# End of the mixing stage in another order: mLSTM scores in the rotary banks, output-weight products between the last heads

## The chip, the cores and the metric

The kernel runs on one core of a Trainium2 chip. The metric is device time in microseconds (us), lower is better: the median over executions.

## The reference, cut to what matters

Two layers of a streaming encoder, 256 tokens, 1024 wide, float32. Each layer has a SwiGLU, a mixing stage, a memory cross-attention and a second SwiGLU, with a layer norm behind each. The mixing stage joins three head groups and multiplies them by one output matrix:

```python
a_out = diff_attention(dq, dk, dv, lam)            # 4 heads, columns 0..511
h = mlstm_chunkwise(q, k, v, ig, lf)               # 4 heads, columns 512..767
b_out = sigmoid(mo) * rms_norm(h, mlstm_norm_g)
c_out = s5_layer(su, ...)                          # columns 768..1023
return jnp.concatenate([a_out, b_out, c_out], -1) @ w_out
```

The memory's keys and values, `mem @ wkv`, do not depend on x and can be computed at any time.

## The kernel before

Every float32 weight block ("unit") of 1 MB (0.5 MB for those in `HALF`) is loaded by SP into one of 5 slots (`RING`), split by ScalarE (ACT) into a high part `WH` and by VectorE (DVE) into a low part `WL` (`split`, once on each engine per unit), and used by TensorE (PE) in three products high x high, high x low, low x high (`prod`). All engines walk through the units in the one order of `unit_order`: unit u is loaded when unit u-5 has been used (`unit_used`), and a `split()` on ACT or DVE always takes the next unit. Each engine is a queue in order; waits are semaphores written by hand.

The end of `mix(l)` on PE works in eight PSUM banks. Banks 0 to 3 become the sum of the output product. `diff_scores`, `diff_turn`, `diff_out` are scores, transposes of probabilities and output of one differential head (heads 0, 1, 3 in banks 6 and 7, head 2 in 4 and 5). `spread` and `decay` give the mLSTM gate matrix `SDA`; `mlstm_scores(h)` multiplies q and k of head h, DVE multiplies that by `SDA` (`decay_scores`, event `msd_ready`), `mlstm_num` multiplies by the values, `mlstm_sums` and `mlstm_scale` (DVE, with a root on POOL) make `CATM` (event `b_ready`). `turn_cat` transposes finished pairs of column blocks, and `cat_high` (ACT) and `cat_low` (DVE) write them to `CH` and `CL`, the inputs of the output product. Output weights are the units W0 (block 6), W1 (block 7), W2 (0, 1), W3 (4, 5), W4 (2, 3). Blocks 6 and 7 are the S5 group, 0 to 3 the heads, 4 and 5 the mLSTM.

`FILL` places products of the memory's keys and values between these steps: in the mixing stage of layer 0 four of them, called `mid` 0 to 3 (units K2, K3, V0, V1); in layer 1 none. `mid_out` evacuates such a product on ACT, and `mid_split(l, i)` is a split that exists in layer 0 alone.

At the end POOL loads the next norm's parameters (`load_gb`, tile `LNGB`), 0.5 MB twice.

Of the kernel before, what the change touches and what calls it, by code (L numbers as in the profile page):

```python
# [35 lines left out]
HEADS = 4  # L36
# [4 lines left out]
TAPS = 4  # L41
# [20 lines left out]
def unit_order():  # L62

    order = []
    for l in range(DEPTH):
        order += [(l, "F0", i) for i in range(FFN_UNITS)]
        order += FILL["mix", l]
        order += [(l, "DV", 0), (l, "DV", 1), (l, "DQ", 0), (l, "DK", 0), (l, "SU", 0), (l, "MQ", 0), (l, "MK", 0),
                  (l, "DQ", 1), (l, "DK", 1), (l, "MM", 0), (l, "MM", 1)]
        mid = FILL["mid", l]  # L70
        order += mid[0:3] + [(l, "W", i) for i in range(4)] + mid[3:4] + [(l, "W", 4)]
        order += FILL["xattn", l]
        order += [(l, "WQ", i) for i in range(4)]
        order += [(l, "WO", i) for i in range(5)]
        order += FILL["ffn2", l]
        order += [(l, "F1", i) for i in range(FFN_UNITS)]
        order += FILL["next", l]
    return order
# [32 lines left out]
def build(nc, x_in, mem_in, wg, wu, wd, ln_g, ln_b, w_in, w_out, wq, wkv, wo, par, const, out):  # L111
# [12 lines left out]
    with ctx:  # L124
# [34 lines left out]
        UT = sb("UT", [P, 2, SEQ])  # L159
# [220 lines left out]
        def _(sp):  # L380
# [59 lines left out]
            for l in range(DEPTH):  # L440
# [11 lines left out]
                for half in range(2):  # L452
                    load_rows(UNIT[l, "MM", half], win_v, l, 4 * half, slice(C_MV, C_MV + 512))
                load_fill("mid", l, 0, 3)
                load_single(UNIT[l, "W", 0], wout_v, l, 6)
                load_single(UNIT[l, "W", 1], wout_v, l, 7)
                load_pair(UNIT[l, "W", 2], wout_v, l, 0)
                load_pair(UNIT[l, "W", 3], wout_v, l, 4)
                load_fill("mid", l, 3, 4)
# [20 lines left out]
        def _(pe):  # L480
# [271 lines left out]
            def mlstm_scores(l, h):  # L752
# [3 lines left out]
                if h < 2:  # L756
                    pe.wait_ge(decay_done.sem, decay_done.at(l, 2 * h + 2))
                else:
                    pe.wait_ge(msd_ready.sem, msd_ready.at(l, h - 1))
                b = h % 2  # L760
                k = COUT[:, 2 + h // 2, :]
# [5 lines left out]
            def mlstm_num(l):  # L767
                pe.wait_ge(msd_ready.sem, msd_ready.at(l, HEADS))
                for t in range(TT):
                    for h in range(HEADS):  # L770
                        o = PS[:, 2 + t, h * 65:h * 65 + 65]
                        if t == 0:
# [105 lines left out]
            def mix(l):  # L878
# [48 lines left out]
                diff_scores(l, 1)  # L927
                cols(l)

                s5_scatter(l)  # L930
                unit_ready(UNIT[l, "MM", 1])
                form_a_tile(UNIT[l, "MM", 1], 1, 0, XH, XL, 0)
                pe.wait_ge(ut_ready.sem, ut_ready.at(l, 2))
                for f in range(2):
# [18 lines left out]
                diff_out(l, 2)  # L953
                diff_scores(l, 3)
                mlstm_scores(l, 2)
                mlstm_scores(l, 3)
                fill_read("mid", l, 1)
                mlstm_num(l)
                diff_turn(l, 3)
                pe.wait_ge(a_ready.sem, a_ready.at(l, 1))  # L960
                pe.wait_ge(do_read.sem, do_read.at(l, 3))
                turn_cat(l, CATA, 0, 5)
                mid(l, 2, 4)
                diff_out(l, 3)

                pe.wait_ge(c_lo.sem, c_lo.at(l, 1))
                pe.wait_ge(num_read.sem, num_read.at(l, 1))
                w = UNIT[l, "W", 0]
                rows_product(w, [6], CH, CL, True, False)
                rows_product(w + 1, [7], CH, CL, False, False)  # L970
                pe.wait_ge(cat_lo.sem, cat_lo.at(l, 1))
                pe.wait_ge(b_ready.sem, b_ready.at(l, 1))
                turn_cat(l, CATM, 0, 5)
                rows_product(w + 2, [0, 1], CH, CL, False, False)
                pe.wait_ge(cat_lo.sem, cat_lo.at(l, 2))
                rows_product(w + 3, [4, 5], CH, CL, False, False)
                fill_read("mid", l, 2)
                mid(l, 3, 4)
                pe.wait_ge(a_ready.sem, a_ready.at(l, 2))
                turn_cat(l, CATA, 2, 7)  # L980
                pe.wait_ge(cat_lo.sem, cat_lo.at(l, 3))
# [91 lines left out]
        def _(act):  # L1073
# [210 lines left out]
            def mix(l):  # L1284
# [41 lines left out]
                split()  # L1326
                act.wait_ge(cols_done.sem, cols_done.at(l, 1))
                copy(SM[:, 184:200], PS[:, 3, 0:16]).then_inc(cols_read.sem, 1)
                diff_exp(l, 1)
# [3 lines left out]
                for f in range(2):  # L1333
                    g = nc.scalar.activation(ZG[:, f, :], PS[:, 2, f * SEQ:f * SEQ + SEQ], ACT.Sigmoid,
                                             bias=PAR[:, P_GLUB + f:P_GLUB + f + 1])
                g.then_inc(glu_sig.sem, 1)
                act.wait_ge(va_ones.sem, va_ones.at(l, 1))
                for t in range(TT):
                    act.wait_ge(unit_used.sem, UNIT[l, "MM", 1] + 1)
                    copy(VA[:, t, :, 0:64], PS[:, t, 0:256].rearrange("p (h d) -> p h d", h=HEADS))  # L1340
                    nc.scalar.activation(SIGO[:, t, :], PS[:, t, 256:512], ACT.Sigmoid).then_inc(mm_read.sem, 1)
                diff_turned(l, 1)
                split()
                diff_exp(l, 2)
                act.wait_ge(cols_read.sem, cols_read.at(l, 1))
# [4 lines left out]
                diff_evac(l, 1)  # L1350
                act.wait_ge(c_hi_in.sem, c_hi_in.at(l, 1))
                copy(CH[:, 6:8, :].rearrange("p f (k s) -> p f k s", s=TAPS),
                     UT[:, :, :].rearrange("p f (s k) -> p f k s", s=TAPS)).then_inc(c_hi.sem, 1)
                split()
                diff_turned(l, 2)
                mid_out(l, 1, 3)
                diff_evac(l, 2)
                split()
                diff_exp(l, 3)
                diff_turned(l, 3)  # L1360
                cat_high(l, 0, 0, 5)
                mid_out(l, 2, 4)
                diff_evac(l, 3)
                mid_split(l, 3)
                cat_high(l, 1, 4, 5)
                split()
                mid_out(l, 3, 4)
                cat_high(l, 2, 2, 7)
                split()
# [73 lines left out]
        def _(dve):  # L1443
# [251 lines left out]
            def decay_scores(l, h):  # L1695

                dve.wait_ge(decay_done.sem, decay_done.at(l, h + 1))
                dve.wait_ge(ms_done.sem, ms_done.at(l, h + 1))
                v.scalar_tensor_tensor(SDA[:, h, :], PS[:, h % 2, 0:384], 0.125, SDA[:, h, :],
                                       ALU.mult, ALU.mult).then_inc(msd_ready.sem, 1)  # L1700

            def mlstm_sums(l):

                dve.wait_ge(num_done.sem, num_done.at(l, 2))
                dve.wait_ge(exp_m.sem, exp_m.at(l, 1))
                n8 = PS[:, 2:4, 0:260].rearrange("p t (h d) -> p t h d", h=HEADS)
                den = SM[:, 120:128]
# [91 lines left out]
            def mix(l):  # L1799
# [48 lines left out]
                diff_combine(l, 2)  # L1848
                diff_max(l, 3)
                decay_scores(l, 2)  # L1850
                decay_scores(l, 3)
                split()
                mlstm_sums(l)
                mlstm_scale(l)
                cat_low(l, 0, 0, 5)
                diff_sums(l, 3)
                diff_combine(l, 3)
                diff_stats(l, 1)
                mid_split(l, 3)
                diff_norm(l, 1)  # L1860
                cat_low(l, 1, 4, 5)
                split()
                cat_low(l, 2, 2, 7)
                split()
# [354 lines left out]
```

## Time and profile before

| | us |
|---|---|
| median of 3 runs (1332.24 to 1340.2) | 1333.86 |
| the profiled execution | 1331.73 |
| its span, first to last instruction | 1329.9 |
| mean granted TensorE clock | 0.986 |
| PE busy | 1266.2 (95%) |
| PE weight load busy | 1084.9 (82%) |
| DVE busy | 772.8 (58%) |
| ACT busy | 590.9 (44%) |

"Busy" is the share of the span in which the engine has an instruction in work. The chain of work that ended last is 72% PE. The mixing stage of layer 0 ends its output product near 398 us, that of layer 1 near 1044 us.

### The profile page before, as it was taken

What the parts mean: (1) busy time and instruction counts of PE and PEld (TensorE: products, weight loads), DVE (VectorE), ACT (ScalarE), POOL (GpSimd) and SP (SyncE); (2) the same over time, 40 slices, a digit from 0 to 9 for tenths busy, and PEclk for the clock granted to TensorE, in tenths of its full rate; (3) what the DMA queues carried; (4) which work ended last, traced back from release to release, by engine and by line L of the source; (5) the groups of instructions that cost most, each with busy time, mean ns of one, the idle gap of its engine ahead of it and who ended that gap; (6) DMA issues with size and microseconds to landing.
All of it is one profiled execution on the core that took longest, in us unless ns stands there. A gap on an engine that the chain in (4) does not pass through costs nothing.

```text
span 1329.9 us, 16421 instructions
## 1 busy us (share of the span) xinstructions
PE 1266.2 (95%) x6896; PEld 1084.9 (82%) x6896; DVE 772.8 (58%) x1003; ACT 590.9 (44%) x670; POOL 151.8 (11%) x153
## 2 busy tenths in 40 slices
PE   6999999999999999999999999999998898999997
PEld 5788888897888888888887878888987796788885
DVE  5577646585545555544556686466747646455543
ACT  5444553456433545444444445544454444344441
POOL 1008800000100000000001088000001000000000
PEclk8999999999899999999999999999999999999999
DMA  8755555421254355555547555545232534455550
GB/s 278 246 186 176 186 183 165 159 96 64 95 191 158 127 190 192 188 190 190 190 158 266 188 174 181 186 159 158 84 107 96 174 112 158 158 190 190 190 189 33
DMA packets 160041, 219.46 MB, mean 165 GB/s; under 512 B 6848, under 2 KB 136000, under 8 KB 159968
## 3 DMA queue, kind: packets, MB, share of 16 engines
q1 hardware_dynamic: 156544, 205.61, 46.2%
q0 software_dynamic: 3152, 11.76, 2.5%
q8 instruction: 54, 0.88, 0.3%
q10 hardware_dynamic: 272, 1.05, 0.2%
q14 instruction: 19, 0.16, 0.0%
HBM read 217.34 MB, written 1.05 MB: 164 GB/s over the span
## 4 chain that ended last, share of the span: by engine, by line
PE 72%; issue 16%; DVE 5%; DMA 3%; ACT 3%; SPq 0%; POOL 0%; DVEq 0%; POOLq 0%; ACTq 0%
PE PS L485 21%; PE PS L487 21%; PE PS L486 21%; DMA RAW<-in_ffn_w_up 2%; DVE WL L1455 1%; ACT WH L1075 1%; PE PS L516 1%; PE PS L996 1%; PE PS L1020 1%; ACT XH L1075 1%; PE PS L553 1%; PE PS L692 1%; DMA RAW<-in_w_out 1%; PE PS L790 0%; DMA RAW<-in_w_in 0%
## 5 line engine op out<-in xcount | busy, mean ns | idle before, releaser
L1455 DVE TENSOR_TENSOR WL<-RAW,WH 128x2048 fp32r<-128x2048 f32 (+1 forms) x198 | 448.3, 2269 | 278.9 <-ACT WH L1075 278.5
L1075 ACT ACTIVATE WH<-RAW 128x2048 fp32r<-128x2048 f32 (+1 forms) x198 | 370.5, 1878 | 182.3 <-DMA RAW<-in_ffn_w_up 132.7
L485 PE MATMUL PS<-WH,XH 128*128 128x512 f32 x768 | 307.4, 400 | 16.2 <-ACT XH L1075 6.5
L487 PE MATMUL PS<-WH,XL 128*128 128x512 f32 x768 | 300.8, 392 | 0.0
L486 PE MATMUL PS<-WL,XH 128*128 128x512 f32 x768 | 300.6, 391 | 0.0
L485 PEld LDWEIGHTS PS<-WH,XH 128*128 128x128 f32 x768 | 145.2, 189 | 47.5 <-issue 10.8
L487 PEld LDWEIGHTS PS<-WH,XL 128*128 128x128 f32 x768 | 144.9, 189 | 30.9
L486 PEld LDWEIGHTS PS<-WL,XH 128*128 128x128 f32 x768 | 145.3, 189 | 28.7 <-issue 0.5
L485 PE MATMUL PS<-WH,HH 128*128 128x512 f32 x352 | 138.7, 394 | 4.6 <-issue 4.6
L486 PE MATMUL PS<-WL,HH 128*128 128x512 f32 x352 | 137.6, 391 | 0.0
L487 PE MATMUL PS<-WH,HL 128*128 128x512 f32 x352 | 137.5, 391 | 0.0
L485 PE MATMUL PS<-XH,WH 128*128 128x256 f32 x352 | 103.7, 295 | 3.2 <-ACT XH L1075 3.2
L486 PE MATMUL PS<-XL,WH 128*128 128x256 f32 x352 | 99.5, 283 | 0.0
L487 PE MATMUL PS<-XH,WL 128*128 128x256 f32 x352 | 99.5, 283 | 0.0
L1075 ACT ACTIVATE HH<-PS 128x512 fp32r<-128x512 f32 x44 | 26.2, 596 | 142.2 <-PE PS L516 142.2
L2098 POOL TENSOR_TENSOR SM<-SM,half_c 128x2 f32<-128x2 f32 x8 | 5.7, 711 | 695.3 <-DVE SM L1507 695.3
L485 PEld LDWEIGHTS PS<-WH,HH 128*128 128x128 f32 x352 | 66.5, 189 | 20.3 <-issue 6.8
L1151 ACT ACTIVATE SG<-PS 128x256 f32<-128x256 f32 x88 | 33.5, 383 | 110.0 <-PE PS L487 109.8
L487 PEld LDWEIGHTS PS<-WH,HL 128*128 128x128 f32 x352 | 66.5, 189 | 14.1
L486 PEld LDWEIGHTS PS<-WL,HH 128*128 128x128 f32 x352 | 66.5, 189 | 13.5
L485 PEld LDWEIGHTS PS<-XH,WH 128*128 128x128 f32 x352 | 67.3, 191 | 5.7 <-ACT XH L1075 3.7
L1455 DVE TENSOR_TENSOR HL<-PS,HH 128x512 fp32r<-128x512 f32 x44 | 30.3, 689 | 69.8 <-ACT HH L1075 69.6
(318 smaller groups left out, 1786.0 us busy)
## 6 DMA issues: line engine op xcount, KB each, us to landing
RAW<-in_ffn_w_gate SPq DMA_DIRECT2D x88, 512.0 KB, 3.8
RAW<-in_ffn_w_up SPq DMA_DIRECT2D x88, 512.0 KB, 4.8
RAW<-in_ffn_w_down SPq DMA_DIRECT2D x88, 512.0 KB, 4.3
RAW<-in_w_in SPq DMA_DIRECT2D x44, 512.0 KB, 4.3
RAW<-in_xattn_wkv SPq DMA_DIRECT2D x32, 512.0 KB, 4.1
RAW<-in_xattn_wq SPq DMA_DIRECT2D x16, 512.0 KB, 3.9
RAW<-in_w_out SPq DMA_DIRECT2D x12, 512.0 KB, 4.4
RAW<-in_xattn_wo SPq DMA_DIRECT2D x12, 512.0 KB, 3.9
```

The source lines that it names most:

```text
L485: nc.tensor.matmul(out_ap, sh, mh, start=first, stop=False)
L486: nc.tensor.matmul(out_ap, sh, ml, start=False, stop=False)
L487: return nc.tensor.matmul(out_ap, sl, mh, start=False, stop=last)
L516: mm = nc.tensor.transpose(PS[:, 6, fc * SEQ + t * P:fc * SEQ + t * P + P], HB[:, t, fc * P:fc * P + P], ident)
L553: mm = nc.tensor.transpose(PS[:, 4 + 2 * t + half, i * P:i * P + P], X[:, t, c * P:c * P + P], ident)
L692: mm = nc.tensor.matmul(PS[0:32, 7, j * P:j * P + P], PCB[:, o:o + 32], CQ[:, part, i, 0:TAPS, :].rearrange("p a c -> p (a c)"), start=(pa ...
L996: mm = nc.tensor.matmul(PS[:, h, t * SEQ:t * SEQ + SEQ], QX[:, 2 * h + c, t * P:t * P + P], KT[:, 2 * h + c, :], start=(c == 0), stop=(c = ...
L1020: mm = nc.tensor.matmul(PS[:, 6 + h % 2, dc * SEQ:dc * SEQ + SEQ], V[:, mt, (2 * h + dc) * P:(2 * h + dc + 1) * P], XPT[:, h % 2, mt, :], ...
L1075: return nc.scalar.activation(dst, src, ACT.Copy)
L1151: nc.scalar.activation(SG[:, t, :], PS[:, 4 + t, 0:FB], ACT.Silu).then_inc(sg_done.sem, 1)
L1455: return v.tensor_tensor(dst, full, hi.bitcast(F32), ALU.subtract)
L2098: g.tensor_tensor(SM[:, 22:24], SM[:, 20:22], half_c[:, 0:2], ALU.pow).then_inc(ln_root.sem, 1)
```

## The change

No operation is added or taken away; they are put in another order and in other banks.

- `mlstm_scores` of heads 2 and 3 go to banks 4 and 5 instead of 0 and 1, and wait for head 2's output to be read; `mlstm_num` goes to 4 and 5 instead of 2 and 3.
- On PE, W0 follows `diff_out(l, 2)`, then the transposes of heads 0 and 1, scores 2 and 3, `diff_scores(l, 3)`, W1, `mlstm_num`, `diff_turn(l, 3)`, the first half of W2, `diff_out(l, 3)`, the transposes of `CATM`, the second half of W2, `mid` 2, half of W3, the last transposes, the other half of W3, `mid` 3, and W4.
- `cols` moves behind the first tile of unit MM 1, and its evacuation on ACT behind the sigmoids.
- The unit V0 moves from before W0 to between W2 and W3, in loads and splits alike.
- On ACT and DVE splits, evacuations, `cat_high`, `cat_low` and the decay products are put in the matching order.

```diff
@@ -70,3 +70,3 @@
         mid = FILL["mid", l]
-        order += mid[0:3] + [(l, "W", i) for i in range(4)] + mid[3:4] + [(l, "W", 4)]
+        order += mid[0:2] + [(l, "W", i) for i in range(3)] + mid[2:3] + [(l, "W", 3)] + mid[3:] + [(l, "W", 4)]
         order += FILL["xattn", l]
@@ -453,3 +453,3 @@
                     load_rows(UNIT[l, "MM", half], win_v, l, 4 * half, slice(C_MV, C_MV + 512))
-                load_fill("mid", l, 0, 3)
+                load_fill("mid", l, 0, 2)
                 load_single(UNIT[l, "W", 0], wout_v, l, 6)
@@ -457,2 +457,3 @@
                 load_pair(UNIT[l, "W", 2], wout_v, l, 0)
+                load_fill("mid", l, 2, 3)
                 load_pair(UNIT[l, "W", 3], wout_v, l, 4)
@@ -758,4 +759,4 @@
                 else:
-                    pe.wait_ge(msd_ready.sem, msd_ready.at(l, h - 1))
-                b = h % 2
+                    pe.wait_ge(do_read.sem, do_read.at(l, 3))
+                b = (0, 1, 4, 5)[h]
                 k = COUT[:, 2 + h // 2, :]
@@ -770,3 +771,3 @@
                     for h in range(HEADS):
-                        o = PS[:, 2 + t, h * 65:h * 65 + 65]
+                        o = PS[:, 4 + t, h * 65:h * 65 + 65]
                         if t == 0:
@@ -927,3 +928,2 @@
                 diff_scores(l, 1)
-                cols(l)
 
@@ -932,2 +932,3 @@
                 form_a_tile(UNIT[l, "MM", 1], 1, 0, XH, XL, 0)
+                cols(l)
                 pe.wait_ge(ut_ready.sem, ut_ready.at(l, 2))
@@ -953,29 +954,31 @@
                 diff_out(l, 2)
-                diff_scores(l, 3)
+                w = UNIT[l, "W", 0]
+                pe.wait_ge(c_lo.sem, c_lo.at(l, 1))
+                pe.wait_ge(msd_ready.sem, msd_ready.at(l, 2))
+                fill_read("mid", l, 1)
+                rows_product(w, [6], CH, CL, True, False)
+                pe.wait_ge(a_ready.sem, a_ready.at(l, 1))
+                turn_cat(l, CATA, 0, 7)
                 mlstm_scores(l, 2)
                 mlstm_scores(l, 3)
-                fill_read("mid", l, 1)
+                pe.wait_ge(cat_lo.sem, cat_lo.at(l, 1))
+                diff_scores(l, 3)
+                rows_product(w + 1, [7], CH, CL, False, False)
                 mlstm_num(l)
                 diff_turn(l, 3)
-                pe.wait_ge(a_ready.sem, a_ready.at(l, 1))
-                pe.wait_ge(do_read.sem, do_read.at(l, 3))
-                turn_cat(l, CATA, 0, 5)
-                mid(l, 2, 4)
+                unit_ready(w + 2)
+                rows_tile(w + 2, [0, 1], CH, CL, 0, False, False)
                 diff_out(l, 3)
-
-                pe.wait_ge(c_lo.sem, c_lo.at(l, 1))
-                pe.wait_ge(num_read.sem, num_read.at(l, 1))
-                w = UNIT[l, "W", 0]
-                rows_product(w, [6], CH, CL, True, False)
-                rows_product(w + 1, [7], CH, CL, False, False)
-                pe.wait_ge(cat_lo.sem, cat_lo.at(l, 1))
                 pe.wait_ge(b_ready.sem, b_ready.at(l, 1))
-                turn_cat(l, CATM, 0, 5)
-                rows_product(w + 2, [0, 1], CH, CL, False, False)
+                turn_cat(l, CATM, 0, 4)
+                rows_tile(w + 2, [0, 1], CH, CL, 1, False, False).then_inc(unit_used.sem, 1)
+                mid(l, 2, 5)
+                w3 = UNIT[l, "W", 3]
+                unit_ready(w3)
                 pe.wait_ge(cat_lo.sem, cat_lo.at(l, 2))
-                rows_product(w + 3, [4, 5], CH, CL, False, False)
-                fill_read("mid", l, 2)
-                mid(l, 3, 4)
+                rows_tile(w3, [4, 5], CH, CL, 0, False, False)
                 pe.wait_ge(a_ready.sem, a_ready.at(l, 2))
-                turn_cat(l, CATA, 2, 7)
+                turn_cat(l, CATA, 2, 6)
+                rows_tile(w3, [4, 5], CH, CL, 1, False, False).then_inc(unit_used.sem, 1)
+                mid(l, 3, 7)
                 pe.wait_ge(cat_lo.sem, cat_lo.at(l, 3))
@@ -1326,4 +1329,2 @@
                 split()
-                act.wait_ge(cols_done.sem, cols_done.at(l, 1))
-                copy(SM[:, 184:200], PS[:, 3, 0:16]).then_inc(cols_read.sem, 1)
                 diff_exp(l, 1)
@@ -1336,2 +1337,4 @@
                 g.then_inc(glu_sig.sem, 1)
+                act.wait_ge(cols_done.sem, cols_done.at(l, 1))
+                copy(SM[:, 184:200], PS[:, 3, 0:16]).then_inc(cols_read.sem, 1)
                 act.wait_ge(va_ones.sem, va_ones.at(l, 1))
@@ -1342,4 +1345,7 @@
                 diff_turned(l, 1)
-                split()
                 diff_exp(l, 2)
+                act.wait_ge(c_hi_in.sem, c_hi_in.at(l, 1))
+                copy(CH[:, 6:8, :].rearrange("p f (k s) -> p f k s", s=TAPS),
+                     UT[:, :, :].rearrange("p f (s k) -> p f k s", s=TAPS)).then_inc(c_hi.sem, 1)
+                split()
                 act.wait_ge(cols_read.sem, cols_read.at(l, 1))
@@ -1350,5 +1356,2 @@
                 diff_evac(l, 1)
-                act.wait_ge(c_hi_in.sem, c_hi_in.at(l, 1))
-                copy(CH[:, 6:8, :].rearrange("p f (k s) -> p f k s", s=TAPS),
-                     UT[:, :, :].rearrange("p f (s k) -> p f k s", s=TAPS)).then_inc(c_hi.sem, 1)
                 split()
@@ -1358,12 +1361,12 @@
                 split()
+                cat_high(l, 0, 0, 7)
                 diff_exp(l, 3)
                 diff_turned(l, 3)
-                cat_high(l, 0, 0, 5)
-                mid_out(l, 2, 4)
+                split()
                 diff_evac(l, 3)
+                cat_high(l, 1, 4, 4)
+                mid_out(l, 2, 5)
+                cat_high(l, 2, 2, 6)
+                mid_out(l, 3, 7)
                 mid_split(l, 3)
-                cat_high(l, 1, 4, 5)
-                split()
-                mid_out(l, 3, 4)
-                cat_high(l, 2, 2, 7)
                 split()
@@ -1698,3 +1701,3 @@
                 dve.wait_ge(ms_done.sem, ms_done.at(l, h + 1))
-                v.scalar_tensor_tensor(SDA[:, h, :], PS[:, h % 2, 0:384], 0.125, SDA[:, h, :],
+                v.scalar_tensor_tensor(SDA[:, h, :], PS[:, (0, 1, 4, 5)[h], 0:384], 0.125, SDA[:, h, :],
                                        ALU.mult, ALU.mult).then_inc(msd_ready.sem, 1)
@@ -1705,3 +1708,3 @@
                 dve.wait_ge(exp_m.sem, exp_m.at(l, 1))
-                n8 = PS[:, 2:4, 0:260].rearrange("p t (h d) -> p t h d", h=HEADS)
+                n8 = PS[:, 4:6, 0:260].rearrange("p t (h d) -> p t h d", h=HEADS)
                 den = SM[:, 120:128]
@@ -1848,5 +1851,6 @@
                 diff_combine(l, 2)
-                diff_max(l, 3)
+                cat_low(l, 0, 0, 7)
                 decay_scores(l, 2)
                 decay_scores(l, 3)
+                diff_max(l, 3)
                 split()
@@ -1854,11 +1858,10 @@
                 mlstm_scale(l)
-                cat_low(l, 0, 0, 5)
                 diff_sums(l, 3)
                 diff_combine(l, 3)
+                cat_low(l, 1, 4, 4)
                 diff_stats(l, 1)
-                mid_split(l, 3)
                 diff_norm(l, 1)
-                cat_low(l, 1, 4, 5)
                 split()
-                cat_low(l, 2, 2, 7)
+                cat_low(l, 2, 2, 6)
+                mid_split(l, 3)
                 split()
```

## Rows read from the trace of the kernel before

**Rows 1.** The page: busy time of TensorE; loads of output weights
```profile
PE 1266.2 (95%) x6896; PEld 1084.9 (82%) x6896; DVE 772.8 (58%) x1003; ACT 590.9 (44%) x670; POOL 151.8 (11%) x153
...
RAW<-in_w_out SPq DMA_DIRECT2D x12, 512.0 KB, 4.4
```

**Rows 2.** Busy time by stretch, PE alone: us, busy, clock, DMA; layers 0, 1
```profile
310.89:392.11 81.22, 75.47 (x496) 0.96 0.35 120
980.19:1037.89 57.70, 51.65 (x303) 0.97 0.34 113
```

**Rows 3.** Timeline of PE, layer 0: start, length, instruction, [idle before <-releaser]
```profile
314.78 0.38 PE L854 MATMUL PS<-kst,RV 4*128 4x4 f32 x4 [1.99 <-DVE DKT L1630]
...
352.96 0.29 PE L773 MATMUL PS<-VA,SDA 128*128 128x65 f32 x1 [1.04 <-DVE SDA L1699]
...
357.05 1.54 PE L825 MATMUL PS<-kst,PR 128*128 128x128 f32 x6 [0.56 <-ACT PR L1232]
...
392.11 0.50 PE L485 MATMUL PS<-WH,CH 128*128 128x512 f32 x1 [1.46 <-DVE CL L1455]
```

**Rows 4.** Timeline of PE, layer 1, same columns
```profile
1001.75 0.70 PE L763 MATMUL PS<-QP,COUT 128*128 128x256 f32 x2 [0.69 <-ACT SDA L1219]
...
1005.76 0.49 PE L833 MATMUL PS<-DV,AT 128*128 128x129 f32 x2 [2.43 <-ACT AT L1075]
...
1037.89 0.50 PE L485 MATMUL PS<-WH,CH 128*128 128x512 f32 x1 [1.41 <-DVE CL L1455]
```

**Rows 5.** Busy by stretch: PE, PEld, DVE, ACT, POOL, then PEclk, the granted clock
```profile
355.00:361.80 6.80, 6.24 (x30) 6.05 (x30) 5.78 (x11) 3.40 (x7) 0.48 (x1) 0.50 0.00 0
1006.90:1010.30 3.40, 3.40 (x11) 2.33 (x10) 2.73 (x9) 0.55 (x3) 0.06 (x1) 0.50 0.87 292
1126.40:1136.60 10.20, 5.75 (x17) 4.61 (x18) 5.88 (x5) 2.40 (x3) 1.50 (x3) 0.50 0.31 106
```

**Rows 6.** Timeline, layer 0, ACT copy and the gate matmuls on PE
```profile
319.06 0.61 ACT L1075 ACTIVATE UT<-PS 128x512 f32<-128x512 f32 x1
...
320.33 1.89 PE L937 MATMUL PS<-UT,PAR 128*128 128x256 f32 x8
```

**Rows 7.** Timeline of PE, layer 0: starts that give the length of pieces
```profile
346.06 0.59 PE L763 MATMUL PS<-QP,COUT 128*128 128x256 f32 x2
...
348.71 0.60 PE L813 MATMUL PS<-DKT,DQT 128*128 128x256 f32 x2
...
367.38 0.47 PE L485 MATMUL PS<-WH,CH 128*128 128x512 f32 x1
...
372.95 0.60 PE L844 MATMUL PS<-kst,CATM 128*128 128x128 f32 x4
```

**Rows 8.** Timeline, layer 0: issues on SP and POOL, the ACT split behind
```profile
346.26 0.81 SPq L389 DMA_DIRECT2D RAW<-in_w_out  x2
...
344.29 0.65 POOL L2042 DMA_DIRECT2D LNGB<-in_ln_g  x1
...
353.84 1.91 ACT L1075 ACTIVATE WH<-RAW 128x2048 fp32r<-128x2048 f32 x1 [3.77 <-DMA RAW<-in_w_out]
```

**Rows 9.** Timeline, layer 1: last of num, its sums on DVE, and their end
```profile
1015.88 0.82 PE L825 MATMUL PS<-kst,PR 128*128 128x128 f32 x6
...
1016.08 0.17 DVE L1709 COPY SM<-PS 128x8 f32<-128x8 f32 x1 [0.79 <-PE PS L776]
...
1021.55 0.69 DVE L1733 TENSOR_TENSOR CATM<-CATM,SM 128x512 f32<-128x512 f32 x1 [1.63 <-POOL SM L2111]
```

**Rows 10.** Timeline, layer 0: evacuation and high parts on ACT, low on DVE
```profile
390.24 0.60 ACT L1075 ACTIVATE V<-PS 128x512 f32<-128x512 f32 x1 [12.98 <-PE PS L487]
...
391.21 5.52 ACT L1075 ACTIVATE WH<-RAW 128x2048 fp32r<-128x2048 f32 x3
...
393.16 6.70 DVE L1455 TENSOR_TENSOR WL<-RAW,WH 128x2048 fp32r<-128x2048 f32 x3 [1.11 <-ACT WH L1075]
```

**Rows 11.** Timeline of DVE, layer 1: the two decay products
```profile
1008.30 1.01 DVE L1699 SCALAR_TENSOR_TENSOR SDA<-PS,SDA 128x384 f32<-128x384 f32 x2
```

More of the change, by code:

```diff
@@ L1342, in mix @@
                 diff_turned(l, 1)
+                diff_exp(l, 2)
+                act.wait_ge(c_hi_in.sem, c_hi_in.at(l, 1))
+                copy(CH[:, 6:8, :].rearrange("p f (k s) -> p f k s", s=TAPS),
+                     UT[:, :, :].rearrange("p f (s k) -> p f k s", s=TAPS)).then_inc(c_hi.sem, 1)
                 split()
-                diff_exp(l, 2)
                 act.wait_ge(cols_read.sem, cols_read.at(l, 1))
@@ L1854, in mix @@
                 mlstm_scale(l)
-                cat_low(l, 0, 0, 5)
                 diff_sums(l, 3)
                 diff_combine(l, 3)
+                cat_low(l, 1, 4, 4)
                 diff_stats(l, 1)
+                diff_norm(l, 1)
+                split()
+                cat_low(l, 2, 2, 6)
                 mid_split(l, 3)
-                diff_norm(l, 1)
-                cat_low(l, 1, 4, 5)
-                split()
-                cat_low(l, 2, 2, 7)
                 split()
```

## The prediction, made before the changed kernel was run

> **What bounds the kernel.** I read the page first: PE is busy 95% of the span [rows 1]. No operation is removed, so all that an order can change is idle time of PE and the time that it runs at half clock. I then asked for the busy time of PE in the two stretches that the change rewrites, from the scores of head 1 to the start of W4, the last output weights [rows 2]: idle 81.22 - 75.47 = 5.75 us in layer 0 and 57.70 - 51.65 = 6.05 us in layer 1. The timeline of PE tells what ends these waits. In layer 0 [rows 3]: 1.99 us for the rotated keys, 1.04 for the decay products, 0.56 for the exponentials of head 3, 1.46 for the last low part; 0.69 more waits for the decay, as in layer 1 [rows 4], where 2.43 is for the turned probabilities of head 2 and 1.41 for the last low part. The granted clock is at its lower level, 1.2 instead of 2.4 GHz, for 6.8 us in layer 0, just after the 1.04 us wait between short matmuls, and for 3.4 us in layer 1, just after the 2.43 us wait [rows 5]. What PE did there took twice as long, so half of its busy time is lost: 3.1 and 1.7 us. Together the stretches hold 5.75 + 3.1 = 8.85 us in layer 0 and 6.05 + 1.7 = 7.75 us in layer 1. That is the most that the change can win: 16.6 us less the decay waits, which it leaves, so about 15, or 1.1%.
>
> **Lengths of the pieces.** A product of one 1 MB unit with both token tiles lasts 372.95 - 367.38 = 5.57 us for two 0.5 MB units, so 2.79 for each such unit or for half of W2 or W3 [rows 7]. Two mLSTM scores and one head's output last 348.71 - 346.06 = 2.65 [rows 7], which I split into 1.31 and 1.34; this split is mine, the sum is the row's. Four transposes of `turn_cat` take 0.35, from the six of `diff_turn`, 0.82 with the tail of the last, so 0.66 by their starts [rows 9].
>
> **Layer 0, the start.** `cols` gets cover: the tile of MM 1 now stands before it, and the 1.99 us wait goes. But the gate matmuls behind that tile wait for ACT's copy of UT, which ended at 319.06 + 0.61 = 319.67 us, when PE came only at 320.33 [rows 6]. That copy stands behind the exponentials of head 1, these behind DVE's maxima, and these behind the split of a unit whose load is issued when MM 0 has been used. None of it moves: the unit is W1 instead of W0, of the same size. So PE comes at about 318.3 and waits 1.4 us. The win is 320.33 - 319.75 = 0.58, not 1.99. The 0.69 us for the decay stays: spread, decay and `mid` 1 keep their order.
>
> **Layer 0, W3's load.** Scores 0 start at 346.06 - 0.58 = 345.48. Then 2.65 (scores, head 2), 2.79 (W0), 0.35 (transposes), 1.31 (scores 2 and 3): PE is at 352.6. Next is `diff_scores(l, 3)`, which now needs bank 7 empty, so `cat_low` 0, so `cat_high` 0 on ACT. In ACT's queue the split of W3 stands ahead of `cat_high` 0, and it waits for W3's load. That load was issued at 346.26 when K3 had been used, shared the time with POOL's parameter loads issued from 344.29 on, and let ACT start at 353.84 [rows 8]. All three shift by the same 0.58: start 353.26, end 355.17, then 0.6 for the copy [rows 10] and 0.7 for the low part, taken as the DVE step of the same size [rows 9], so PE goes on at 356.5. New wait: 3.9 us. DVE's decay products of heads 2 and 3 queue behind the same `cat_low`, but W1 covers them.
>
> **Both layers, the normalised mLSTM output.** From the end of `mlstm_num` (1016.0) to the end of the last DVE step (1021.55 + 0.69 = 1022.24) the sums, POOL's root and the scaling take 6.2 us [rows 9]. Before, W0 and W1 covered them. Now between `mlstm_num` and the transposes of `CATM` stand only `diff_turn` 0.66, half of W2 2.79 and `diff_out` 1.34, 4.8 us. New wait: 1.5 us in each layer.
>
> **Layer 0, the split of W4.** The units' order fixes which unit each split takes. In layer 0 the splits of ACT from the decay on are V0, W3, V1 and, as `mid_split(l, 3)`, W4; and this last one now stands behind `mid_out(l, 3, 7)`, the evacuation of V1's product. PE does V1 immediately before W4. So after V1's last matmul: evacuation 0.5 (390.24 to the next start), the high part 1.92 (its end is where DVE starts, 393.16 - 391.21 = 1.95), the low part 6.70 / 3 = 2.2, the hand-over 0.1 [rows 10]. New wait: 4.8 us, in place of the 1.46 us there. W3's halves cannot cover it, being ahead of V1. In layer 1 there is no `mid` 3; W4's split stands at the place before head 3's evacuation, early enough, and the last low part is ready just as W3's second half ends: the 1.41 us goes.
>
> **Layer 1, the decay products.** W0 waits for `msd_ready` 2. DVE's two products ended at 1008.30 + 1.01 = 1009.31 [rows 11], behind the split of W2 and the norm of heads 0 and 1, and that order is kept; ACT's decay starts up to 0.4 later, as a split and the S5 copy now stand ahead of it. I take 1009.6 for them and 1002.0 for scores 0 (1001.75 before [rows 4], decay wait 1.0 instead of 0.69). PE needs 2.65 for scores and head 2, so it idles 4.8 of the 7.6 us (with the tail of the last matmul). No `mid` product lies here, other than in layer 0. Then 0.15 for `cat_low` 0, since W3 is loaded long before, and the 1.5 us from above: 1.0 + 4.8 + 0.15 + 1.5 = 7.4 us idle.
>
> **The clock.** The new waits are longer than those after which it fell. The rows do not show a fall after 3.9 or 4.8 us, so I bound it: 0 below; above, 10.2 us at half, as after the longest wait of the trace [rows 5], of which the wait itself covers a part. Between, 6.8 us that begin inside the wait: about 4 us of work at half, 2 us lost, nearest to the first of [rows 5]. I take 2.0 for each of the two long waits of layer 0 and 1.3 for layer 1, where the fall begins inside a longer broken stretch.
>
> The Trainium skill (TensorE: Matmul & The Clock Gate, HAM oscillation) ties the fall to long idle gaps of the array. The trace agrees for the 2.43 us wait and less for the first fall, after 1.04 us of idle among short matmuls. By the rule alone layer 1's broken waits might cost no fall, and the sum would be 1.3 us lower.
>
> **The sum.** Layer 0: waits 1.4 + 0.7 + 3.9 + 1.5 + 4.8 = 12.3, clock 4.0, so 16.3 against 8.85: +7.5 us. Layer 1: waits 7.4, clock 1.3, so 8.7 against 7.75: +0.9 us. In all +8.4. The SP queue issues the same loads; moving V0 behind W2 lets W2 load one unit earlier, which nobody waits for. The layer norm behind W4 has the same fillers and starts no later after W4. The profiled execution would go from 1331.7 to 1340.1 us; it lies 2.1 below the median of 1333.86, so the median goes to 1342.
>
> **Rivals.** (a) The clock stays up in the new waits: -5.3, 1337 us. For it: 1.99 us of idle at 314.78 [rows 3] brought no fall, as the 6.8 us at half account for the whole of the mean 0.96 [rows 2]. Against: a wait half as long did. (b) W3's load lands sooner, at the page's 4.4 us after its second issue [rows 1]: near 350.6, so the wait is 1.0 instead of 3.9 and its fall of the clock goes: -4.9, 1337 us. For it: the parameter loads might lie elsewhere; against: POOL's issue hangs on the same chain and shifts with it. (c) Slower by over 1%: the clock stays low until dense work has run for long, 10.2 us at each of four waits (the two in layer 0, the one at the decay products and the one before `CATM`), with about 7 us of work in each: 3.5 lost at each, 14 instead of 5.3, so 1351 us. It decides from some 10.5 us lost to the clock on. Against: only one stretch of 10.2 in the trace, with 6 us idle. (d) Faster: W4's and W3's splits do not stand where I count them, because ACT is a unit ahead; then every new wait is covered and only the decay waits remain: 16.6 - 1.4 = 15.2 saved, 1319 us. It decides from the point where V1's evacuation no longer stands ahead of the low part of W4. Against: in the profile the split at 353.84 waits for the output weights' load, W3, which fixes the count.
>
> **Numbers.** The forecast 0.60, (a) 0.14, (b) 0.11, (c) 0.10, (d) 0.05. Predicted 1342 us. The range 1335 to 1348 holds the forecast, (a), (b) and the lower edge of (c). About 1% is what a measurement can tell from no change: 1320.5 to 1347.2 is "the same". Faster: (d) less its doubt, 0.04. Slower: (c), 0.09. Within: 0.87.
>
> **What the profile after would show.** Right: in layer 0 a wait of PE near 4 us ahead of `diff_scores(l, 3)`, ended by DVE's `CL`; one of 1.5 ahead of the `CATM` transposes, ended by DVE's `CATM`; one near 4.8 ahead of W4, ended by DVE's `WL`; the clock at 0.5 behind the first and the third; a wait on ACT's UT copy at the gate matmuls. In layer 1 waits ended by DVE's `SDA` ahead of W0. Wrong: W4 starting right after V1 in layer 0, W3's split not waiting for a load, or a stretch of layer 1 with less idle than 6 us.

## The result: 1.0064 times the time before, and the profile after

| | before | changed | ratio, 95% interval |
|---|---|---|---|
| median of 9 runs each, us | 1334.06 | 1343.08 | 1.0064 [1.0049, 1.0079] |
| profiled execution: span, us | 1329.9 | 1340.3 | |
| mean granted clock | 0.986 | 0.984 | |

The change makes the kernel 9 us slower, inside the 1% that was called "the same". The forecast was 1342. The page after shows the same work as before [rows 1]:

```profile
PE 1269.8 (95%) x6896; PEld 1086.8 (81%) x6896; DVE 771.8 (58%) x1003; ACT 590.4 (44%) x670; POOL 150.5 (11%) x153
```

Busy time of PE by stretch, from near the scores of head 1 to the start of W4, in layer 0 and in layer 1 (length, busy, clock, DMA share, GB/s), answers to [rows 2]:

```profile
310.89:398.55 87.66, 76.20 (x496) 0.95 0.38 126
989.20:1046.52 57.32, 50.32 (x303) 1.00 0.34 111
```

Layer 0's stretch is 6.4 us longer, layer 1's 0.4 shorter. The timeline of PE after, answering to [rows 3] (layer 0, first four) and [rows 4] (layer 1), shows in brackets how long PE waits now and which instruction ended the wait. "Issue" means that the profile names none; what the wait of 2.88 us is for is settled by an experiment below:

```profile
320.19 0.48 PE L938 MATMUL PS<-UT,PAR 128*128 128x256 f32 x1 [1.45 <-ACT UT L1078]
...
356.24 0.80 PE L814 MATMUL PS<-DKT,DQT 128*128 128x256 f32 x1 [2.91 <-DVE CL L1458]
...
372.79 0.33 PE L845 MATMUL PS<-kst,CATM 128*128 128x128 f32 x1 [1.52 <-DVE CATM L1736]
...
398.55 0.76 PE L486 MATMUL PS<-WH,CH 128*128 128x512 f32 x1 [4.90 <-DVE WL L1458]
...
1011.37 0.48 PE L764 MATMUL PS<-QP,COUT 128*128 128x256 f32 x1 [1.10 <-ACT SDA L1222]
...
1014.38 0.38 PE L834 MATMUL PS<-DV,AT 128*128 128x129 f32 x1 [1.44 <-ACT AT L1078]
...
1018.87 0.47 PE L486 MATMUL PS<-WH,CH 128*128 128x512 f32 x1 [2.88 <-issue]
...
1037.35 0.33 PE L845 MATMUL PS<-kst,CATM 128*128 128x128 f32 x1 [1.48 <-DVE CATM L1736]
```

None of the waits of [rows 3] is left; four others have come, together 10.8 us instead of 5.1. The clock is at half in three stretches of these stages (columns PE, PEld, DVE, ACT, POOL busy, granted clock, DMA), two in layer 0 and one at the layer norm behind layer 1's mixing stage, answering to [rows 5]. Such a stretch at half clock is called a fall from here on:

```profile
355.50:362.30 6.80, 6.06 (x14) 4.35 (x15) 3.82 (x7) 0.98 (x4) 0.00 (x0) 0.50 0.11 39
396.50:403.30 6.80, 4.75 (x11) 3.80 (x12) 6.80 (x4) 4.98 (x3) 0.00 (x0) 0.50 0.22 76
...
1068.90:1072.30 3.40, 3.40 (x18) 3.40 (x17) 2.29 (x1) 0.47 (x1) 0.00 (x0) 0.50 0.00 0
```

The third comes just after waits of 1.32 and 1.62 us at the norm. The kernel before has the same two waits there and no fall; the second of them, in the trace before and in the trace after:

```profile
1060.02 0.36 PE L485 MATMUL PS<-XH,WH 128*128 128x256 f32 x1 [1.62 <-ACT XH L1075]
...
1068.51 0.36 PE L486 MATMUL PS<-XH,WH 128*128 128x256 f32 x1 [1.62 <-ACT XH L1078]
```

The two longest waits are explained by the queues of ACT and DVE. At W3 the split at the head of ACT's queue waits 3.04 us for the load, which SP issues while POOL's parameter loads are under way, and the high part of the first head blocks stands behind that split. At W4 the order is evacuation of V1, high part, low part:

```profile
344.24 0.65 POOL L2045 DMA_DIRECT2D LNGB<-in_ln_g  x1
346.21 0.82 SPq L389 DMA_DIRECT2D RAW<-in_w_out  x2
353.07 1.91 ACT L1078 ACTIVATE WH<-RAW 128x2048 fp32r<-128x2048 f32 x1 [3.04 <-DMA RAW<-in_w_out]
354.88 0.58 ACT L1078 ACTIVATE CH<-PS 128x512 fp32r<-128x512 f32 x1
...
355.50 0.69 DVE L1458 TENSOR_TENSOR CL<-PS,CH 128x512 fp32r<-128x512 f32 x1 [4.83 <-ACT CH L1078]
...
393.69 0.60 ACT L1078 ACTIVATE V<-PS 128x512 f32<-128x512 f32 x1 [7.90 <-PE PS L488]
394.18 1.90 ACT L1078 ACTIVATE WH<-RAW 128x2048 fp32r<-128x2048 f32 x1
...
396.12 2.29 DVE L1458 TENSOR_TENSOR WL<-RAW,WH 128x2048 fp32r<-128x2048 f32 x1 [9.60 <-ACT WH L1078]
```

Where the 10.4 us of span went, by the starts of the same PE instructions in both timelines: 8.6 up to the first cross-attention score of layer 0; 0.4 in the feed-forwards behind it; -0.5 to the end of layer 1's mixing stage; 1.5 in the half-clock stretch at 1068.9; 0.4 at the end.

### The profile page after: what moved, and what is told of

Same layout as the page of the kernel before. It is cut to its first block, busy times and chain, and to the rows that moved or that the text cites. A ratio compares the mean times of both kernels' runs of the same rounds, so it can differ in the third digit from the quotient of the medians.

```text
span 1340.3 us, 16416 instructions
## 1 busy us (share of the span) xinstructions
PE 1269.8 (95%) x6896; PEld 1086.8 (81%) x6896; DVE 771.8 (58%) x1003; ACT 590.4 (44%) x670; POOL 150.5 (11%) x153
## 4 chain that ended last, share of the span: by engine, by line
PE 71%; issue 16%; DVE 5%; ACT 3%; DMA 3%; POOL 0%; SPq 0%; DVEq 0%; POOLq 0%; ACTq 0%
PE PS L486 21%; PE PS L488 21%; PE PS L487 21%; DMA RAW<-in_ffn_w_up 2%; DVE WL L1458 2%; ACT WH L1078 1%; PE PS L517 1%; PE PS L999 1%; PE PS L1023 1%; DMA RAW<-in_w_out 1%; ACT XH L1078 1%; PE PS L554 1%; PE PS L693 1%; PE PS L791 1%; PE PS L814 1%
## 5 line engine op out<-in xcount | busy, mean ns | idle before, releaser
L486 PEld LDWEIGHTS PS<-WH,XH 128*128 128x128 f32 x768 | 145.3, 189 | 47.6 <-issue 10.5
```

Of the source, the lines that this page charges most:

```text
L486: nc.tensor.matmul(out_ap, sh, mh, start=first, stop=False)
```

## The experiments

All are the changed kernel with a small edit, timed beside the kernel before. One question is whether each wait has the cause that was read, the other what the clock adds.

### W4's split ahead of V1's evacuation

```diff
                 cat_high(l, 2, 2, 6)
-                mid_out(l, 3, 7)
                 mid_split(l, 3)
+                mid_out(l, 3, 7)
```

> The changed kernel, with one line of ACT moved: in layer 0 the split of W4 stands before the evacuation of V1's product instead of behind it. Theory (the 4.90 us wait before W4 comes from that place, and the fall of the clock at 396.5 comes from the wait): the wait goes, W4 runs at full clock, so 4.9 + 2.4 = 7.3 us less than the changed kernel, near 1336 us, ratio to before 1.001. Rival A (the low part waits for W4's load or for DVE, not for the place of the split): a wait of 2 us or more ended by DVE's WL stays, ratio 1.003 or more. Rival B (the clock falls there for another reason than the wait): the wait goes but the half clock near 396 stays, so about 4.9 us less, ratio 1.003.

Measured: 1341.9 us, ratio 1.0048 [1.0029, 1.0067]. No wait ahead of W4 is left in the trace, and no half clock within 20 us of it. Yet the median is only 1.2 us below the changed kernel's, or 2.1 us by the ratios, since the kernel before was slower beside it too (1335.64 us instead of 1334.06). The cause of the wait was right, the price expected was not, so both kernels were run again on one chip.

> The changed kernel once more, beside the one below. It serves two questions. How far do executions of one program differ in where the clock falls: if the falls are tied to the waits alone, this trace has those at the two long waits of layer 0, none at the gate matmuls (near 320) and one near 1069, as the first trace of it; if the moment decides too, some are missing or others appear, while all waits are as long as before within 0.2 us. Ratio to before 1.006.

> The kernel with W4's split ahead of V1's evacuation once more, on the same chip as the changed one. Its first measurement gave 1.2 us instead of 7.3. Theory now: the wait and the fall behind it are really gone (7.3), but 0.7 is given back before the layer norm, since the splits of V2, V3 and WQ0 still stand behind V1's evacuation and hold DVE until 6.7 us after it, so that the norm's low parts are late; the rest was lost to falls of the clock at other places of that execution. Then this run is 3 to 6.5 us below the changed one. Rival: the 7.3 us are given back in every execution: 0 to 2 us below the changed one.

Measured: changed kernel 1345.53 us, 1.0066 [1.0042, 1.0090]; with the edit 1340.93 us, 1.0034 [1.0020, 1.0048]: 4.6 us apart by the medians, 4.3 by the ratios. That is inside what was expected, and less than the 7.3 of the wait and its clock. The trace of the edit's second run shows a part given back. DVE still waits for ACT's three other splits behind V1's evacuation, so the norm's steps come later against PE, a split stands ahead of the norm's low parts, and PE waits 2.36 us there instead of 1.62:

```profile
397.94 6.70 DVE L1458 TENSOR_TENSOR WL<-RAW,WH 128x2048 fp32r<-128x2048 f32 x3 [6.21 <-ACT WH L1078]
404.55 1.22 DVE L1497 SCALAR_TENSOR_TENSOR X<-PS,X 128x1024 f32<-128x1024 f32 x1
...
413.30 2.29 DVE L1458 TENSOR_TENSOR WL<-RAW,WH 128x2048 fp32r<-128x2048 f32 x1
415.51 2.48 DVE L1458 TENSOR_TENSOR XL<-PS,XH 128x512 fp32r<-128x512 f32 x4
...
418.08 0.55 PE L486 MATMUL PS<-XH,WH 128*128 128x256 f32 x1 [2.36 <-issue]
```

The second part is the clock. The same execution has it at half at five places in and behind the two stages. The changed kernel's first trace has only the second and the fifth of them; not the first, at the gate matmuls, the third, at the norm, and the fourth, at layer 1's W0:

```profile
322.30:325.70 3.40, 3.40 (x13) 2.78 (x12) 0.02 (x1) 1.48 (x4) 0.00 (x0) 0.51 0.00 0
359.90:363.30 3.40, 3.40 (x10) 2.17 (x9) 0.99 (x3) 0.00 (x0) 0.00 (x0) 0.50 0.03 9
417.90:421.30 3.40, 3.21 (x15) 3.25 (x16) 2.38 (x2) 0.31 (x1) 0.00 (x0) 0.50 0.26 75
1015.20:1018.60 3.40, 2.76 (x7) 2.21 (x8) 1.47 (x6) 2.41 (x3) 0.00 (x0) 0.51 0.57 157
1066.40:1069.80 3.40, 3.02 (x14) 3.05 (x15) 2.40 (x2) 1.24 (x1) 0.00 (x0) 0.51 0.11 42
```

And the changed kernel's own second trace differs from its first: the clock is at half near 1021 (W0) and not near 1069, though the waits there are the same within 0.1 us; there is one more near 423.7, at layer 0's norm, behind the same two waits as before; and at W3 the stretch is 3.4 us long instead of 6.8, though the wait is 4.36 instead of 2.91:

```profile
1021.10:1024.50 3.40, 3.40 (x9) 2.65 (x9) 0.61 (x2) 2.06 (x3) 0.00 (x0) 0.51 0.12 39
1069.00:1072.40 3.40, 1.78 (x15) 1.57 (x16) 1.40 (x3) 2.82 (x3) 0.00 (x0) 1.00 0.70 255
```

So the length of the wait alone does not decide whether the clock falls; what else does, these traces do not show. Of the 7.3 us expected, 0.7 came back at the norm, which the trace shows. That falls elsewhere took the rest is an inference from two traces of each kernel, since the other runs left none.

### The first head blocks' high part ahead of W3's split

```diff
                 diff_evac(l, 2)
-                split()
                 cat_high(l, 0, 0, 7)
+                split()
```

> The changed kernel, with ACT's high part of the first two head blocks (cat_high 0) taken before the split of W3 instead of behind it. Theory: the wait of 2.91 us before the scores of head 3 in layer 0 comes from the load of W3 that ACT waits for at the head of its queue; it falls to 0.3 us or less, and with it the fall of the clock at 355.5 (6.06 us of busy PE at half, 3.0 lost): 2.6 + 3.0 = 5.6 us less, near 1337.5 us, ratio 1.002. Rival (the transposes, scores and DVE's low part take that long anyway): a wait of over 2 us stays, ratio 1.006.

Measured: 1338.79 us, ratio 1.0026 [1.0014, 1.0037]. PE no longer waits ahead of the scores of head 3: the last scores before them start at 353.76, they at 354.68, while ACT's split still waits for the load. The clock stays up there. The theory held, and the rival is out.

```profile
353.31 0.60 ACT L1078 ACTIVATE CH<-PS 128x512 fp32r<-128x512 f32 x1 [2.03 <-PE PS L845]
354.37 1.91 ACT L1078 ACTIVATE WH<-RAW 128x2048 fp32r<-128x2048 f32 x1 [0.47 <-DMA RAW<-in_w_out]
...
354.68 0.70 PE L814 MATMUL PS<-DKT,DQT 128*128 128x256 f32 x2
```

### The norm's parameters loaded later

```diff
-                load_gb(l, 1)
                 root_ml(l)
+                load_gb(l, 1)
```

> The changed kernel, with POOL's two loads of the next norm's parameters (1 MB) issued behind the root of the mLSTM sums instead of before it, so that W3's load has the DMA engines to itself. Theory: W3 lands 4.8 us after its issue instead of 6.8, the wait before the scores of head 3 falls from 2.91 to about 0.9 us, and the clock then may not fall: 2.0 to 5 us less than the changed kernel, ratio 1.003 to 1.005. Rival (the load is slow by itself or by HBM): it lands after 6.5 us or more, no change, ratio 1.006. A second rival: the parameters come too late for the norm, and a new wait stands before DVE's first norm step.

Measured: 1340.53 us, ratio 1.0030 [1.0014, 1.0046], with no new wait at the norm. W3's load is issued at 348.09 and lets ACT start at 352.93, 4.8 us; in the changed kernel it took from 346.21 to 353.07, 6.9 us, beside POOL's two. The wait falls from 2.91 to 0.90. The parameter loads are 2 us of it.

```profile
348.09 0.81 SPq L389 DMA_DIRECT2D RAW<-in_w_out  x2
...
352.93 1.91 ACT L1078 ACTIVATE WH<-RAW 128x2048 fp32r<-128x2048 f32 x1 [1.02 <-DMA RAW<-in_w_out]
...
356.11 0.48 PE L814 MATMUL PS<-DKT,DQT 128*128 128x256 f32 x1 [0.90 <-DVE CL L1458]
```

### Layer 1's decay products first

```diff
+                if l == 1:
+                    decay_scores(l, 0)
+                    decay_scores(l, 1)
                 split()
                 diff_norm(l, 0)
-                decay_scores(l, 0)
-                decay_scores(l, 1)
+                if l == 0:
+                    decay_scores(l, 0)
+                    decay_scores(l, 1)
```

> The changed kernel, with DVE's decay products of mLSTM heads 0 and 1 taken in layer 1 before the split of W2 and the norm of heads 0 and 1, instead of behind them; layer 0 as it was. Theory: the wait of 2.88 us before W0 in layer 1 is for these products, which stand behind 3.3 us of other work on DVE; it falls below 0.3 us: 2.7 us less, near 1340.4 us, ratio 1.0045. Rival A (it is for the evacuation or the low part of the S5 columns): the wait stays, ratio 1.006. Rival B: the norm of the heads is then late and a wait as long stands before the transposes behind W0, ratio 1.006.

Measured: 1343.31 us, ratio 1.0056 [1.0036, 1.0077], which can't be told from the changed kernel's. The trace shows the theory and a part of rival B: the wait of 2.88 before W0 is gone, so it was for the decay products, and two others of together 1.85 us stand behind W0, because DVE reads head 2's output, which frees the bank of the next scores, only after split and norm:

```profile
1022.30 0.48 PE L764 MATMUL PS<-QP,COUT 128*128 128x256 f32 x1 [1.06 <-DVE CATA L1768]
...
1024.66 0.48 PE L814 MATMUL PS<-DKT,DQT 128*128 128x256 f32 x1 [0.79 <-DVE CL L1458]
```

### W2 whole before the mLSTM transposes

```diff
                 diff_out(l, 3)
+                rows_tile(w + 2, [0, 1], CH, CL, 1, False, False).then_inc(unit_used.sem, 1)
                 pe.wait_ge(b_ready.sem, b_ready.at(l, 1))
                 turn_cat(l, CATM, 0, 4)
-                rows_tile(w + 2, [0, 1], CH, CL, 1, False, False).then_inc(unit_used.sem, 1)
```

> The changed kernel, with the second half of W2 taken before PE waits for the normalised mLSTM output, instead of behind the transposes of it. Theory: the wait of 1.5 us before those transposes goes in both layers, since 2.8 us of product cover it. In layer 0 V0's product covers what follows; in layer 1 the transposes' own high and low part (0.35 + 0.6 + 0.7) are then uncovered and bring 1.3 us back: 1.5 + 0.2 = 1.7 us less, ratio 1.005. Rival: what follows is late in layer 0 too, ratio 1.006.

Measured: 1345.86 us, ratio 1.0058 [1.0035, 1.0082], against 1.0066 of the changed kernel in the same session, which tells nothing of 1.7 us. In the trace the waits of 1.5 before `CATM` are gone in both layers; in layer 1 one of 1.50 for the low part and one of 0.21 have come behind it, in layer 0 none. So layer 1 loses 0.2 us by it and layer 0 wins 1.5. The mechanism is shown, its worth in time is not: this execution also has a fall at 727.2, far from the edit, and one of 13.7 us at 1140.2 where the changed kernel's first trace has 10.2.

```profile
1044.12 0.47 PE L486 MATMUL PS<-WH,CH 128*128 128x512 f32 x1 [1.50 <-DVE CL L1458]
...
1047.34 0.33 PE L845 MATMUL PS<-kst,CATA 128*128 128x128 f32 x1 [0.21 <-DVE CATA L1789]
```

### cols back at its old place

The four transposes on PE and their copy on ACT return to where the kernel before has them.

```diff
                 diff_scores(l, 1)
+                cols(l)
...
                 form_a_tile(UNIT[l, "MM", 1], 1, 0, XH, XL, 0)
-                cols(l)
```

> The changed kernel, with the four transposes of cols and their evacuation back at their old places. One look; the trace of layer 0 decides. The prediction held that cols waited 1.99 us for the rotated keys and that its new place takes that wait away, all but 1.4 us of it coming back at the gate matmuls. Theory now, from the changed kernel's trace: the rotated keys are ready 2 us sooner anyway, since the split before them on DVE is now half a unit (W0 instead of V0); with cols back its wait is 0.7 us or less, the gate matmuls still start when ACT's copy of UT ends, 1.1 to 1.5 us after PE is ready in all, and the move of cols alone is worth 0. Rival: the wait before cols is about 2 us again and the gate matmuls start 0.5 us later against the scores of head 1.

One run alone, 1342.98 us, so only the trace counts. `cols` follows the scores of head 1 without a wait (313.17, 313.49), and the gate matmuls wait 1.47 us as with the move. They start 9.0 us after the scores of head 1, with `cols` at either place.

```profile
313.17 0.39 PE L816 MATMUL PS<-kst 128*128 128x128 f32 x2
313.49 0.41 PE L855 MATMUL PS<-kst,RV 4*128 4x4 f32 x4
...
320.70 0.48 PE L938 MATMUL PS<-UT,PAR 128*128 128x256 f32 x1 [1.47 <-ACT UT L1078]
```

The line of DVE in the changed kernel that writes the rotated keys tells why:

```profile
310.99 1.39 DVE L1633 TENSOR_TENSOR DKT<-ZT,ZS 64x512 f32<-64x512 f32 x2
```

They are ready at 312.4, where before `cols` could start only at 314.78 [rows 3], since the split in front of them is now half a unit, 1.2 us on DVE instead of 2.3, and ACT's half is sooner done too. The move of `cols` is worth nothing; the move of V0 took its wait away.

### All waits at once, and a version faster than both

`cat_high` 0 ahead of W3's split; W2 whole; in layer 0 the splits of W4, V2 and V3 ahead of V1's evacuation, with a wait of PE for that evacuation before the bank is filled again; and for layer 1 an order of its own:

```diff
+                fill_read("mid", l, 3)
                 fill("xattn", l)
...
                 cat_high(l, 2, 2, 6)
-                mid_out(l, 3, 7)
                 mid_split(l, 3)
                 split()
                 split()
+                mid_out(l, 3, 7)
                 split()
...
                 diff_evac(l, 1)
+                if l == 1:
+                    diff_turned(l, 2)
                 split()
-                diff_turned(l, 2)
+                if l == 0:
+                    diff_turned(l, 2)
...
-                split()
-                diff_norm(l, 0)
+                if l == 0:
+                    split()
+                    diff_norm(l, 0)
                 decay_scores(l, 0)
                 decay_scores(l, 1)
+                if l == 1:
+                    diff_norm(l, 0)
                 diff_sums(l, 2)
                 diff_combine(l, 2)
                 cat_low(l, 0, 0, 7)
                 decay_scores(l, 2)
                 decay_scores(l, 3)
+                if l == 1:
+                    split()
```

> The changed kernel with all waits taken on at once: cat_high 0 before W3's split; W2 whole before the mLSTM transposes; W4's, V2's and V3's splits before V1's evacuation in layer 0 (PE waits for that evacuation before it fills the bank again); in layer 1 decay products, norm and head 2's sums before W2's low part on DVE, and the turned probabilities of head 2 before W2's split on ACT. Theory: layer 0 keeps waits of 1.45, 0.7 and 0.2 us against 5.75 before, and no 6.8 us at half clock (3.1); layer 1 keeps 1.1, 0.1, 0.9, 0.2 and 1.3 us against 6.05, and no 3.4 us at half clock (1.7): 6.5 + 4.1 = 10.6 us below the kernel before if the clock never falls in the two stretches, 5 us below it if it falls for 3.4 us at three places. Ratio 0.992 to 0.996. Rival (each wait that is removed comes back as a later one): ratio 0.999 or more.

Measured: 1327.66 us, ratio 0.9934 [0.9915, 0.9953]. In the rewritten stretches layer 0 keeps only the decay's wait and that at the gate matmuls, layer 1 waits of 1.11, 1.36, 1.50 and 0.21 us. The last addition takes on the gate matmuls' wait, which comes from a load that ACT awaits some 40 us before PE uses it:

```diff
-                split()
                 diff_exp(l, 1)
                 act.wait_ge(g4_done.sem, g4_done.at(l, 1))
                 copy(UT[:, :, :], PS[:, 2, :].rearrange("p (f n) -> p f n", f=2)).then_inc(ut_ready.sem, 1)
+                split()
...
-                split()
                 diff_max(l, 1)
+                split()
```

> The kernel with all waits taken on at once, once more, as the partner of the next one on the same chip. Its first trace had falls of the clock near 321 (3.4 us, at the gate matmuls) and 410 (6.8 us, at the layer norm behind the mixing stage). Ratio 0.992 to 0.995.

> The kernel with all waits taken on, and besides the split that stands before the exponentials of head 1 (W1 in layer 0, W0 in layer 1) moved behind them and behind the copy of UT on ACT, and behind the maxima of head 1 on DVE. Theory: the wait of 1.45 to 1.57 us before the gate matmuls of layer 0 is for W1's load, for which ACT waits 3.4 us at the head of its queue though W1 is used 35 us later; the wait goes, and the fall of the clock that some executions have there: 1.5 to 3.2 us less than its partner, ratio 0.990 to 0.992. Rival (the exponentials and the copy are late for themselves): the wait stays over 1 us, no difference.

Measured: without the addition 1322.37 us, 0.9912 [0.9881, 0.9942]; with it 1322.97 us, 0.9908 [0.9882, 0.9934]. The wait is gone: the gate matmuls start at 319.54 behind the last `cols` at 319.20, and PE is busy 85.2 of 86 us of layer 0's stretch at full clock. The medians don't tell the two apart, where 1.5 to 3.2 us were expected, so the 1.5 us are shown in the trace alone.

```profile
319.20 0.41 PE L855 MATMUL PS<-kst,RV 4*128 4x4 f32 x4
319.54 1.78 PE L938 MATMUL PS<-UT,PAR 128*128 128x256 f32 x7
...
310.00:396.00 86.00, 85.20 (x571) 1.00 0.43 141
```

## Why the prediction was right, point by point

- **W4's split in layer 0**, forecast 4.8 us: 4.90, ended by DVE's `WL`. Right in cause (the edit removes it) and size.
- **W3's load**, forecast 3.9: 2.91 in the profiled execution, since the load took 6.9 us from issue to split instead of the 7.6 of [rows 8]. In the six other traces that keep this order the wait is 2.82 to 4.36, so the size varies from execution to execution. Rival (b), a load that lands after the profile page's 4.4 us, did not come; with the parameter loads out of the way it took 4.8. The cause is shown twice, by the order on ACT and by the parameter loads.
- **The mLSTM output**, forecast 1.5 in each layer: 1.52 and 1.48.
- **Layer 1's decay products**, forecast 4.8 in one piece and 1.0 for the decay: 1.10, 1.44 and 2.88, together 5.4 against 5.8. Only the 2.88 is for the decay products; the 1.44 is for ACT's turned probabilities of head 2, the rest of the 2.43 of [rows 4], which the prediction had put under the same term. The sign it gave, waits ended by DVE's `SDA` ahead of W0, can't be read off the profile, which says "issue"; the edit shows it. The stretch is 0.4 shorter where 0.4 shorter was forecast if the clock stayed up (7.4 against 7.75).
- **The start of layer 0**, forecast a wait of 1.4 and a win of 0.58: a wait of 1.45 and a win of 0.4, since the gate matmuls start 9.0 us after the scores of head 1 instead of 9.4; by the mLSTM scores of head 0 it is 0.3. The reason given was wrong in one step. The prediction let the move of `cols` take away the wait for the rotated keys; in fact the moved unit V0 had already done so, by making the split ahead of the keys half as long. The prediction followed the moved unit in ACT's queue and not in DVE's.
- **The pieces**: four transposes of `turn_cat` take 0.44 us (351.42 to 351.86), not 0.35; six of them take 0.66 in the prediction's own row. It changes nothing else.
- **The clock**, forecast 2.0 lost at each long wait of layer 0 and 1.3 in layer 1: half of the busy time at the lower level is 3.0 and 2.4, and nothing in layer 1's stretch. The sum of 5.3 against 5.4 is partly luck: in the second trace the falls lie elsewhere. Rival (a), in which the clock stays up, is out, and so is rival (c): no fall in the two stages is longer than 6.8 us, and none stands at the wait before `CATM`. The 1.5 us lost at 1068.9, behind waits of 1.32 and 1.62 us that the kernel before has too, were in no term.
- **The sum**: +8.4 forecast; +10.4 for the span of the profiled execution, +9.0 for the medians, interval +6.5 to +10.5. That it is so near is luck in part. Layer 0 cost 8.6 us up to its first cross-attention score where 7.5 was forecast, layer 1 won 0.5 where a loss of 0.9 was forecast, and 2.3 us lie outside both stages, where the forecast had nothing.
- **The faster rival**, (d) (W4's and W3's splits stand elsewhere), is out: both stand where they were counted.

## What to carry to other kernels

In a pipeline in which every engine takes units in one fixed order, write down for each engine which unit every split takes after a reorder, and look for a split that has come to stand behind an evacuation of the product just before its own use: that is a serial chain (here 4.9 us), whatever the average load of the engines. A wait for a load at the head of a queue holds all that stands behind it; put what the bound engine needs next ahead of it. And go on until no long wait is left: single edits gave 1 to 5 us by the ratios, all together 17 to 20 against the changed kernel (ratios to before of 0.9934 and 0.9912 instead of 1.0064). The single gains at the four waits add up to some 9 to 12. That removing them together is worth more than their sum is not shown, since the last two versions also hold steps that were not run alone.

## What the runs showed of the hardware

A single wait of PE of about 1.5 us among short matmuls can be followed by a clock of 1.2 GHz for 3.4 us, and about the same wait in another execution of the same program is not: of the eleven traces with the wait at the gate matmuls, four have the fall there and seven don't. In the four the wait is 1.52 to 1.57 us, in the seven 1.40 to 1.49; whether these hundredths matter is not shown. Only the longest waits have it each time: the waits of 2.8 to 4.4 us at layer 0's W3 have it in seven traces of seven, the 2.9 us at layer 1's W0 in three of eight, the 1.32 and 1.62 at layer 1's norm in eight of thirteen. The runs of the kernel before on one chip go from 1332.19 us at a mean clock of 0.988 to 1340.13 us at 0.980, though one of 1340.05 us has 0.984, so the clock is not all of the spread. The falls shown for these stages cost 1.4 to 3.1 us each, taken as half of PE's busy time in them, behind waits of 1.0 to 4.9 us. With such a spread medians can't judge an edit of under 2 us; the waits in a trace can. The Trainium skill (TensorE: Matmul & The Clock Gate, HAM oscillation) names long idle gaps as the danger; the traces agree for 4.9 us of idle, where all seven that have the wait have the fall, and show falls after much shorter ones as well.
